# Two-block sequence model in float32: another order for the mixers of the first block, and the first sixteen weight loads issued ahead

## The reference, cut to what matters

```
mod = silu(c) @ ada_w[l] + ada_b[l]                # six vectors of 1024
h = rmsnorm(x) * (1 + sc_m) + sh_m
proj = h @ w_in[l]                                 # 1024 x 2824
out_a = sliding window attention (8 heads, window 128) of proj
out_b = hgrn2 recurrence (4 heads, chunks) of proj
out_c = gated delta rule (4 heads, chunks) of silu(conv(proj)):
        T = inverse of (eye + A);  U = T @ ..., W = T @ ...
        then a scan over the chunks: v_new = u - w @ state; o = ...; state = ...
x = x + gt_m * (concat(out_a, out_b, out_c) @ w_out[l])
x = x + gt_f * swiglu(rmsnorm(x) * (1 + sc_f) + sh_f)
```

## Time and profile before

| | |
|---|---|
| median of 3 runs | 4436.93 us (4436.51 to 4437.48) |
| profiled execution, its own time | 4433.45 us |
| its span | 4431.7 us |
| PE busy | 4051.1 us, 91% |
| DVE busy | 2573.7 us, 58% |
| ACT busy | 1639.0 us, 37% |
| mean granted TensorE clock | 0.945 of full speed |
| chain that ended last | PE 75%, DVE 15%, ACT 6%, DMA 2% |

### The profile page before, as it was taken

How to read it: one execution, slowest core, us unless ns; L and a number is a source line. 1 busy time by engine, 2 the same in 40 slices (tenths; PEclk the granted TensorE clock), 3 DMA queues, 4 the chain that set the end, 5 groups by cost and what they waited for, 6 DMA issues and landing times.

```text
span 4431.7 us, 51774 instructions
## 1 busy us (share of the span) xinstructions
PE 4051.1 (91%) x20660; PEld 3326.6 (75%) x20660; DVE 2573.7 (58%) x4060; ACT 1639.0 (37%) x2880; POOL 107.7 (2%) x199
## 2 busy tenths in 40 slices
PE   5878979988879899999999999999899999999998
PEld 4757868867659778888888777767778787777776
DVE  6775455554675332346666744676566667445865
ACT  2343232233443232333434233453344343334532
POOL 0000000000000000000000000000000000000000
PEclk9978889999979799989999999999899999999999
DMA  6402135633202133323231233133242312231233
GB/s 219 148 15 67 44 119 189 191 124 96 72 10 77 58 95 96 98 93 105 81 105 58 81 91 91 53 108 119 70 132 78 109 60 84 81 91 62 78 105 121
DMA packets 216641, 417.93 MB, mean 94 GB/s; under 512 B 16384, under 2 KB 61472, under 8 KB 214608
## 3 DMA queue, kind: packets, MB, share of 16 engines
q1 hardware_dynamic: 197584, 335.12, 24.4%
q0 software_dynamic: 18816, 79.49, 5.2%
HBM read 378.89 MB, written 35.67 MB: 94 GB/s over the span
## 4 chain that ended last, share of the span: by engine, by line
PE 75%; DVE 15%; ACT 6%; DMA 2%; issue 2%; DVEq 0%; SPq 0%; ACTq 0%; POOLq 0%
PE ps L570 55%; PE ps L103 14%; DVE arena L120 4%; ACT arena L191 3%; PE ps L109 3%; DVE arena L135 3%; DVE spl L120 3%; PE ps L2142 2%; ACT sph L191 1%; DMA ring<-in_ada_w 1%; DVE sm L141 1%; DVE HF L120 1%; DVE X L120 1%; PE ps L2138 1%; DVE arena L129 0%
## 5 line engine op out<-in xcount | busy, mean ns | idle before, releaser
L120 DVE TENSOR_TENSOR spl<-ring,sph 128x1024 fp32r<-128x1024 f32 (+2 forms) x556 | 651.6, 1179 | 834.7 <-ACT sph L191 833.3
L191 ACT ACTIVATE sph<-ring 128x1024 fp32r<-128x1024 f32 (+2 forms) x556 | 562.2, 1021 | 878.6 <-PE ps L570 668.2
L570 PE MATMUL ps<-sph,HTh 128*128 128x512 f32 (+3 forms) x1728 | 685.5, 397 | 10.7 <-ACT sm L191 5.4
L570 PE MATMUL ps<-spl,HTh 128*128 128x512 f32 (+3 forms) x1728 | 638.6, 370 | 0.0
L570 PE MATMUL ps<-sph,HTl 128*128 128x512 f32 (+3 forms) x1728 | 637.5, 369 | 0.0
L191 ACT ACTIVATE arena<-ps 128x512 f32<-128x512 f32 (+2 forms) x574 | 316.9, 564 | 778.6 <-PE ps L570 479.2
L570 PE MATMUL ps<-HTh,sph 128*128 128x512 f32 x1376 | 548.4, 399 | 23.1 <-DVE spl L120 16.0
L570 PE MATMUL ps<-HTh,spl 128*128 128x512 f32 x1376 | 540.1, 393 | 0.0
L570 PE MATMUL ps<-HTl,sph 128*128 128x512 f32 x1376 | 540.0, 392 | 0.0
L103 PE MATMUL ps<-arena 64*128 64x128 f32 (+7 forms) x2328 | 410.5, 368 | 55.7 <-ACT arena L191 22.3
L570 PE MATMUL ps<-sph 128*128 128x512 f32 x992 | 402.4, 406 | 8.8 <-DVE spl L120 8.7
(11 more groups left out here) (195 smaller groups left out, 5293.6 us busy)
## 6 DMA issues: line engine op xcount, KB each, us to landing
ring<-in_w_in SPq DMA_DIRECT2D x264, 512.0 KB, 3.7
ring<-in_ada_w SPq DMA_DIRECT2D x96, 512.0 KB, 4.4
ring<-in_w_down SPq DMA_DIRECT2D x44, 512.0 KB, 3.3
ring<-in_w_gate SPq DMA_DIRECT2D x40, 512.0 KB, 4.2
ring<-in_w_up SPq DMA_DIRECT2D x40, 512.0 KB, 4.6
ring<-in_w_mem SPq DMA_DIRECT2D x32, 512.0 KB, 3.4
ring<-in_w_out SPq DMA_DIRECT2D x32, 512.0 KB, 3.7
ring<-in_w_br_ssd SPq DMA_DIRECT2D x32, 512.0 KB, 3.8
```

The source lines that it names most:

```text
L120: self.e.tensor_tensor(o, a, b, op).then_inc(*self.done.up())
L191: self.e.activation(o, a, f, **kw).then_inc(*self.done.up())
L570: ins = pe.e.matmul(o, l, r, start=k0 == 0 and i == 0 and not b.pairs, stop=k0 + b.ks == b.kt and i == 3 * b.ks - 1 and (c0 > 0 or not b.p ...
```

## The change

It touches four things.

1. **Early loads.** The first 16 chunks (EARLY, the whole of the phase ada0) get a place of their own each, eight in HF and eight in the arena, and a semaphore of their own each; SP issues them without any wait. c and c1 are still loaded first, cst goes behind chunk 3, x behind chunk 5, pos behind chunk 15. The next three chunks use the ring, unwaited as well. xsave waits for the last of the first four vectors (mod, 0, 3). The gates of norm0 move from slots 8 and 10 to 10 and 12.
2. **inv no longer comes after att.** As long as att is not over in the plan, the inversion takes banks 3, 0 and 1 and its recurrence 2, 3, 0 and 1; once it is over, the pools are as before.
3. **hgrn stops before its step 8** until att is over: of its fourteen levels the last twelve then come behind attention. Its gate moves from slot w + 4 to slot w.
4. **Another rule in weave** from the end of "hvb" on (turn): a step of the chain (gdn, inv) that is due by q.t + 1.5 goes first; else one step of the other sides, but not two in a row; else a slot of main, if its gate is met; else the side step that is due first.

Both layers of the first model use it. The diff, cut to its core:

```diff
+EARLY = 16
+        early_in = [sem(f"early_in{i}") for i in range(EARLY)]
-                     inv=(3, 4, 5), state=(2, 3, 4, 5))
+                     inv=(3, 4, 5), state=(2, 3, 4, 5), inv_early=(3, 0, 1), state_early=(2, 3, 0, 1))
-        def weave(q, phase, main, sides, gates=()):
+        def weave(q, phase, main, sides, gates=(), chain=(), turn=1 << 30):
...
+            def soon(names, when):
+                return pick([(d, n) for d, n in can() if d <= when and n in names])
+
+            others = [n for n, _, _, _ in sides if n not in chain]
             while "main" not in over:
+                if slot >= turn:
+                    who = soon(chain, q.t + SLACK)
+                    if who is None and plan[-1] not in others:
+                        who = soon(others, q.t + SLACK)
+                    if who is None and all(met(x) for x in gates.get(slot, ())):
+                        who = "main"
+                    if who is None:
+                        go_on()
+                        continue
+                    step(who)
+                    slot += who == "main"
+                    continue
...
         def ring(c):
-            return view(RG[c["id"] % RING], c["b"].ks, c["b"].nw)
+            i = c["id"]
+            if i < EARLY:
+                z = HFx[:, 1024 * i:1024 * i + 1024] if i < 8 else AR[:, 1024 * i - 2048:1024 * i - 1024]
+                return z.rearrange("p (a b) -> p a b", a=KS)
+            return view(RG[i % RING], c["b"].ks, c["b"].nw)
...
-            at["in", "cst"] = s.move(ld["cst"], cst[:, :], T["cst"][:, 0:K_NF])
-            at["in", "x"] = s.move(ld["x"], X[:, :, :], T["x"].rearrange("o (m p) d -> p (o m) d", p=128))
-            at["in", "pos"] = s.move(ld["pos"], pos[:, :], T["pos"])
+        def later_sp(s, n):
+            if n == 4:
+                at["in", "cst"] = ...
+            elif n == 6:
+                at["in", "x"] = ...
+            elif n == EARLY:
+                at["in", "pos"] = ...
...
+            past.add(("att", l))
...
+            def pool(name):
+                return name if ("att", l) in past else name + "_early"
...
-                      ("hgrn", (), {0: slot_after(name, ("hzb", l, 1)), 22: slot_after(name, ("hvb", l, 1))}),
-                      ("inv", ("gdn", "att"), 0), ("mem", ("att",), 0),
+                      ("hgrn", (), {0: slot_after(name, ("hzb", l, 1)), 8: ("att", 99), 22: slot_after(name, ("hvb", l, 1))}),
+                      ("inv", ("gdn",), 0), ("mem", ("att",), 0),
...
+        CHAIN = ("gdn", "inv")
...
-            return {slot_after(k, ("hvb", l, 1)): [("mem", 99)], w + 4: [("hgrn", 99)], w + 8: [("inv", 99)]}
+            return {slot_after(k, ("hvb", l, 1)): [("mem", 99)], w: [("hgrn", 99)], w + 8: [("inv", 99)]}
...
-                q.wait_ge(*[at[x] for x in old])
+                q.wait_ge(*[at[x] for x in old], at["mod", 0, 3])
...
-                      {1: [("norm", 1)], 8: [("norm", 2)], 10: [("norm", 99)]})
+                      {1: [("norm", 1)], 10: [("norm", 2)], 12: [("norm", 99)]})
...
-            weave(q, k, main(q, k), mixers(q, l), mix_gates(l))
+            weave(q, k, main(q, k), mixers(q, l), mix_gates(l), CHAIN, slot_after(k, ("hvb", l, 1)))
...
-                s.wait_ge(at["ring_read", c["id"] - RING] if c["id"] >= RING else None)
+                later_sp(s, c["id"])
+                s.wait_ge(at["ring_read", c["id"] - RING] if c["id"] >= EARLY + RING else None)
```

More of the change, by code:

```diff
@@ L337, in program @@
         at = Marks()
-        bank_of, plans = {}, {}
+        bank_of, plans, past = {}, {}, set()
         POOLS = dict(gemm=(0, 1, 2, 3), side=(4, 5, 6, 7), main=(0, 1), gdn=(2, 3), att=(4, 5), hgrn=(6, 7), xm=(2,), wout=(0, 1, 6, 7),
                      seg=(4, 5), yd=(6,), low=(4, 5), high=(6, 7), last=(7,),
-                     inv=(3, 4, 5), state=(2, 3, 4, 5))
+                     inv=(3, 4, 5), state=(2, 3, 4, 5), inv_early=(3, 0, 1), state_early=(2, 3, 0, 1))
         lane = dict.fromkeys(POOLS, 0)
         held_by = {}
+        HFx = HF.rearrange("p a b -> p (a b)")
         ident = cst[:, K_ID:K_ID + 128]
@@ L663, in start_sp @@
             at["in", "c1"] = s.move(ld["c1"], c1s[:, :, :], T["c1"].rearrange("l p n -> p l n"))
-            at["in", "cst"] = s.move(ld["cst"], cst[:, :], T["cst"][:, 0:K_NF])
-            at["in", "x"] = s.move(ld["x"], X[:, :, :], T["x"].rearrange("o (m p) d -> p (o m) d", p=128))
-            at["in", "pos"] = s.move(ld["pos"], pos[:, :], T["pos"])
+        def later_sp(s, n):
+            if n == 4:
+                at["in", "cst"] = s.move(ld["cst"], cst[:, :], T["cst"][:, 0:K_NF])
+            elif n == 6:
+                at["in", "x"] = s.move(ld["x"], X[:, :, :], T["x"].rearrange("o (m p) d -> p (o m) d", p=128))
+            elif n == EARLY:
+                at["in", "pos"] = s.move(ld["pos"], pos[:, :], T["pos"])
         def start_pool(p):
@@ L1465, in inv_pe @@
                     lv, m = INV[s - 1]
-                    b1 = take(pe, ("t1", l, s - 1), "inv")
-                    b2 = take(pe, ("t2", l, s - 1), "inv") if lv < 6 else None
+                    b1 = take(pe, ("t1", l, s - 1), pool("inv"))
+                    b2 = take(pe, ("t2", l, s - 1), pool("inv")) if lv < 6 else None
                     pe.wait_ge(at["xm", l, s - 1])
@@ L1476, in inv_pe @@
             for m in range(4):
-                bank = take(pe, ("nw", l, m), "state")
+                bank = take(pe, ("nw", l, m), pool("state"))
                 pe.wait_ge(at["tt", l, 20 + m])
@@ L1484, in inv_pe @@
             for half in range(2):
-                bank = take(pe, ("qt", l, half), "state")
+                bank = take(pe, ("qt", l, half), pool("state"))
                 for u in range(4):
@@ L1491, in inv_pe @@
                 if m < 4:
-                    b, b2, b3 = take(pe, ("vn", l, m), "state"), take(pe, ("og", l, m), "state"), take(pe, ("sg", l, m), "state")
+                    b, b2, b3 = [take(pe, (n, l, m), pool("state")) for n in ("vn", "og", "sg")]
                     pe.wait_ge(at["nw", l], at["qt", l])
@@ L2909, in sp_program @@
                     w, n0 = b.w, b.n0
-                at["ring", c["id"]] = s.move(ring_in[c["id"] % RING], ring(c),
+                at["ring", c["id"]] = s.move(early_in[c["id"]] if c["id"] < EARLY else ring_in[c["id"] % RING], ring(c),
                                              w[k0 * 128:(k0 + b.ks) * 128, n0:n0 + b.nw].rearrange("(k p) n -> p k n", p=128))
@@ L2922, in program @@
         held_by.clear()
+        past.clear()
         for s in sems:
```

## The result

The median of the kernel after is 4394.09 us (4385.71 to 4400.48, 4 runs) against 4437.20 beside it: a ratio of 0.9902 [0.9884, 0.9919], faster by 43 us. The forecast was 4308 (4250 to 4392), so the direction holds and the size does not: the gain is a third of the 129 us forecast, and the median lies 2 us outside the range. The profiled execution took 4395.62 us, 37.8 less than before's.

What follows compares the result with a forecast made beforehand. Each layer was taken as bound by DVE and waits, then PE, then the recurrence alone. Two layers at -57 (-114) and the start (-15) from 4433.45 gave 4304.5 profiled, 4308 median, range 4250 to 4392.

Steps and rivals of the forecast that it cites:

- The start, -15: Early loads of ada_w: last of the four vectors at about 37 us instead of 52.5; -15 us, ends -10 and -18.
- by bytes: Start estimate from total bytes: 11.6 MB at 379 GB/s take 30.6 us, with landing and last chunk's work 37.
- The inversion's wait: Inversion's wait for attention: removing it is worth nothing by itself, as gdn, ending at 386.5 us, is what is late.
- The first stretch, 146.5 to 91: Last w_in matmul to gdn's end: 43 us of DVE work leave, 70.5 stay, at the same 78% DVE share 91 us.
- the rival of the clock: First stretch: PE's 53 us of full-clock work runs at half clock, 107 us; layer gains 41, time 4340; 10%.
- The third stretch has filler now and runs at full clock: Recurrence joined to the inversion's stretch: levels, hgrn's tail and main slots fill it; 175 us of PE work take 177.
- the 8 us for the memory load: Allowance added after gdn because the memory tokens' load is less covered and ACT, DVE and the inversion queue behind it.
- the 185 forecast for this stretch: Inversion and recurrence as one PE-bound stretch: 177 us plus 8 for the memory load, against 186.5 before.
- the filler is gone before the recurrence: Rival: main slots run out during the inversion, the 57 us tail stays; 216 us after gdn, -26 a layer, 4370; 13%.
- Attention did not starve: Rival that attention starves under chain-first order with main shut: layer 351 us against 333, time 4458; 4%.
- three signs of being wrong: DVE's share under 65% before the first mask; recurrence alone near clock 0.5; memory load later, counted from last w_in matmul.
- the sign for being right: After the first mask, PE at 98% and full clock until w_out, with recurrence steps between main slots.

Runs made afterwards that it cites:

- e1: The changed kernel with the mixers' order as before, so only the early loads; 4430.52 us against 4435.94, ratio 0.9987.
- e3: The kernel before with only the inversion's wait for attention removed (and its early banks); 4438.40 us, ratio 1.0006.
- e5: The changed kernel with 24 of mv's slots kept until inv step 25 as filler for the recurrence; 4406.95 us, ratio 0.9938.
- e6: The changed kernel with w_out wholly behind the inversion, so the recurrence has nothing beside it; 4405.20 us, ratio 0.9927.
- e8: The changed kernel with 24 main slots kept until inv step 25 and three main slots between recurrence steps; 4380.08 us, ratio 0.9871.
- e10: The changed kernel with 16 slots kept, two main slots between recurrence steps, the other slots spread over the inversion; 4373.43 us, ratio 0.9857.
- e12: As e10, with x also asked for behind chunk 10 of ada_w instead of behind chunk 5; 4374.66 us, ratio 0.9857.
- e7: The kernel before with hgrn's twelve levels held behind attention and its gate at w, old rule of turns; 4442.52 us, ratio 1.0014.

## Why the prediction was wrong

**The start, -15, came as -9.6 in the trace (-8.9 in the mean of all traces) and -5.4 in the time of e1.** Chunk 0 was there at 6.0 us (5.5 forecast), and the DMA was faster than the 379 GB/s I took:

```profile
10.00:15.00 5.00, 0.29 (x2) 0.32 (x2) 4.25 (x6) 0.45 (x3) 0.00 (x0) 1.00 1.04 402
15.00:20.00 5.00, 1.54 (x8) 1.46 (x7) 2.74 (x4) 0.26 (x2) 0.00 (x0) 1.00 1.03 406
```

The step that failed is "by bytes", as a single total. I asked when the last byte comes and when DVE would be done if it never waited, and took the later. DVE waits before that: 2.8 us for the first chunk, 2.5 for the second, 1.3 for the fifth, and 4.9 for the seventh, behind x. From 23.7 on it works without a gap until the last chunk, so what it lost by then stays lost. A server that is fed in order ends at the latest of (arrival of chunk n + the work from n on), and here that is the chunk behind x: 23.7, ten chunks in 16.1 us, and 3.8 for the norm and modt, 43.6.

**The inversion's wait** was worth nothing by itself (e3). Right.

**The first stretch, 146.5 to 91, came as 100.** The work taken out was right, since DVE has 72.2 us left (70.5 forecast). The 78% was the wrong term: it is 72%. The chain of gdn has waits of its own that no levels fill any more, the longest the 7.28 us at 267.87, where ACT does four exponentials for attention and six copies for gdn ahead of the small function that DVE wants. PE's clock was 0.76, its work 50 us at full clock where the rival of the clock had 53. That rival needs PE busy at half clock throughout (107 us); PE was busy for 66.4 of 100.4 us.

**"The third stretch has filler now and runs at full clock"** is the step that failed, and with it went 36 of the 45 us by which a layer missed. From gdn's end to the recurrence's PE is busy for 109.04, 44.68 and 55.65 us at 0.98, 0.89 and 0.64, which is 182 us of work at full clock; I had 175. Of the 218.6 us that it took, 209.4 are busy and 9 idle. So the stretch lost 27 us to the clock, where I allowed none, and 9 to waits, where I allowed 2; the 8 us for the memory load did not come at all (a wait of 0.16). The 36 are these 27.1, and 7.2 of waits, 7.2 of work and 2.4 behind the recurrence that I had not, less the 8. Of the 27, 20 are lost in the recurrence (55.65 us at 0.64), as many as before. Two things are wrong in that sentence. The filler is not there: mv's slots are gone by 446 and the gate at w holds the next until 486. And filler of one slot at a time hardly lifts the clock: 0.64 with it in after and e5, 0.56 without in e6. Two or three at a time do, 0.86 to 0.94 in e8 to e10. That is worth 10 to 16 of the 27 us a layer (e10 and e12). No run comes near the 185 forecast for this stretch, since 182 us of it are work even at full clock.

What the layer gained follows from this. The levels, hgrn's tail and the slots moved out of the first stretch are PE work too, 34 us by the earlier trace rows and the windows of after (182 less 148.6), and they came to lie where PE was already full, as e7 shows by itself. I had 26 of these 34, but paid for them with 21 us of clock and 11 of waits in the third stretch that were never given back: over the whole, 27 us were lost to the clock (24 before) and 9 to waits (14 before). The 46 us won before the inversion less the 34 by which the rest grew are the 12 that a layer gained.

**The rivals.** The nearest was "the filler is gone before the recurrence" (4370, 13%). It names the right place, and its 216 us for what follows gdn lie near the 222 measured (330.4 to the first main slot behind the inversion, 552.5). What it missed is the first stretch's other 9 us and the start. Attention did not starve: the memory load is issued 114.3 us after the last w_in matmul, 124.6 before.

**The signs.** None of the three signs of being wrong came as I had written them: DVE's share is 72% and not under 65, the memory load comes earlier, and the recurrence runs at 0.64 with single slots, not alone. What failed is the sign for being right, PE at 98% and full clock until w_out; its absence should have stood among the others.

**What would have shown it beforehand.** The row was there: PE busy for 45.75 of 57 us at a clock of 0.55. I read the 20% of gaps as the cause and supposed that filling them lifts the clock. After has the recurrence at 19.31 of 20 us busy and 0.59.

## What to carry to other kernels

Moving work out of a stretch that another engine bounds gains only if the place it goes to has room on every engine it uses; count it there before counting the gain. A chain of small matmuls at the lower clock is a reserve of its own: try keeping two or more blocks of wide matmuls for each gap in it instead of letting one block fall into each. Here one left the clock at 0.64, two or three gave 0.86 to 0.94, and the same 1504 matmuls took 10 to 16 us less. And for a stage fed by a queue, work out the end from each arrival, not from the last byte.

## What was not expected of the hardware

- **A busy TensorE at half clock.** 19.31 of 20 us busy at a granted clock of 0.59, with groups of matmuls of 64 columns and single blocks of six of 512 columns between them. With two blocks at a time (twelve of 256 columns each, or six of 512) the same chain had 0.94, with PE busy for 96% (67.55 of 70.2 us). The Trainium skill, in TensorE: Matmul & The Clock Gate (Part 1), has the clock released by how busy PE has been; if busy is what the profile counts, this trace does not agree. What it is about the short matmuls that makes the difference is open: it wasn't tried.
- **A single block of main at 1.2 GHz takes 2.83 to 2.86 us against 1.43**, double, and still nearly seven slots lengthen the recurrence of after by no more than 8.5 us. Only four of them ran so; beside them the recurrence's own waits shrink by 3 us (8.0 in e6, 5.2 in after), and a few of its pieces behind one come at full clock (1.27 at 508.22).
- **The DMA queue read at 402 and 406 GB/s** with nothing being stored, where the earlier trace rows had 440 with a store in the mixture.
